# Stick-breaking sums as products of two halves: a two-layer decoder trunk on one core

## The reference

```python
z = jnp.einsum('bqhd,bkhd->bhqk', q[:, q0:kl], k[:, :kl]).astype(jnp.float32) * scale
mask = s_pos < t_pos
log_stay = jnp.where(mask, jax.nn.log_sigmoid(-z), 0.0)
between = lax.cumsum(log_stay, axis=3, reverse=True) - log_stay
a = jnp.where(mask, jnp.exp(jax.nn.log_sigmoid(z) + between), 0.0)
outs.append(jnp.einsum('bhqk,bkhd->bqhd', a.astype(v.dtype), v[:, :kl]))
...
```

## Time and profile before

| | |
|---|---|
| median of 3 runs | 1400.66 us (1398.6 to 1401.35) |
| the profiled execution | 1401.09 us, span of its instructions 1398.8 us |
| TensorE matmul busy | 1379.2 us (99%) |
| VectorE busy, ScalarE busy | 1137.6 us (81%), 933.0 us (67%) |
| TensorE's granted clock, mean | 0.995 of full |
| the two stretches with the changed steps | 64 to 112 us and 364 to 412 us |

### The profile page before, as it was taken

The page is one execution under the profiler, slowest core; times in us unless marked ns, Lnnn a source line. Parts: engine busy times, 40 slices in busy tenths (PEclk is TensorE's granted clock), DMA queues, the critical chain, the costliest instruction groups (busy, mean ns, idle before and its releaser), DMA issues.

```text
span 1398.8 us, 19126 instructions
## 1 busy us (share of the span) xinstructions
PE 1379.2 (99%) x7313; PEld 1172.1 (84%) x7313; DVE 1137.6 (81%) x872; ACT 933.0 (67%) x751; POOL 35.8 (3%) x53
## 2 busy tenths in 40 slices
PE   9999999999999999999999999999999999999986
PEld 8888999889888888888888888888888888888765
DVE  6866565556857998988888888898888888888897
ACT  5555443445645777777777777777777777777775
POOL 0010000000010020000000000000000000000200
PEclk9999999999999999999999999999999999999998
DMA  9734985546424999999999999999999999999993
GB/s 333 278 106 152 398 321 182 197 164 204 157 92 149 350 371 395 396 394 397 387 394 395 356 385 394 373 370 387 391 357 395 389 370 375 394 389 351 397 394 153
DMA packets 191039, 448.78 MB, mean 321 GB/s; under 512 B 8516, under 2 KB 11275, under 8 KB 190987
## 3 DMA queue, kind: packets, MB, share of 16 engines
q1 hardware_dynamic: 189162, 441.74, 86.1%
q0 software_dynamic: 1616, 5.77, 1.1%
q10 hardware_dynamic: 208, 0.54, 0.1%
HBM read 429.67 MB, written 18.36 MB: 320 GB/s over the span
## 4 chain that ended last, share of the span: by engine, by line
PE 88%; DVE 5%; DMA 3%; issue 1%; ACT 1%; SPq 1%; DVEq 0%; ACTq 0%
PE ps L551 81%; DVE w_lo L386 4%; DMA raw<-in_expert_w_up 2%; PE ps L1010 2%; ACT w_hi L381 1%; PE ps L682 1%; DMA raw<-in_w_in 1%; PE ps L713 0%; PE ps L969 0%; PE ps L736 0%; PE ps L640 0%; PE ps L671 0%; PE ps L556 0%; PE ps L935 0%; PE ps L980 0%
## 5 line engine op out<-in xcount | busy, mean ns | idle before, releaser
L386 DVE TENSOR_TENSOR w_lo<-raw,w_hi 128x2048 fp32r<-128x2048 f32 x401 | 914.5, 2290 | 186.7 <-ACT w_hi L381 186.0
L381 ACT ACTIVATE w_hi<-raw 128x2048 fp32r<-128x2048 f32 x400 | 766.4, 1918 | 296.5 <-PE ps L551 276.4
L551 PE MATMUL ps<-w_hi,xe_hi 128*128 128x512 f32 x896 | 244.8, 395 | 0.0
L551 PE MATMUL ps<-w_lo,xe_hi 128*128 128x512 f32 x896 | 240.1, 390 | 0.1
L551 PE MATMUL ps<-w_hi,xe_lo 128*128 128x512 f32 x896 | 240.0, 390 | 0.0
L551 PEld LDWEIGHTS ps<-w_hi,xe_lo 128*128 128x128 f32 x896 | 168.2, 188 | 35.9
L551 PEld LDWEIGHTS ps<-w_lo,xe_hi 128*128 128x128 f32 x896 | 167.9, 188 | 36.2 <-DVE w_lo L386 0.9
L551 PEld LDWEIGHTS ps<-w_hi,xe_hi 128*128 128x128 f32 x896 | 164.6, 188 | 31.7
L551 PE MATMUL ps<-w_lo,he_hi 128*128 128x512 f32 x448 | 121.4, 392 | 5.7 <-DVE w_lo L386 5.5
L551 PE MATMUL ps<-w_hi,he_hi 128*128 128x512 f32 x448 | 121.1, 391 | 0.5 <-DVE he_hi L1921 0.5
L551 PEld LDWEIGHTS ps<-w_lo,he_hi 128*128 128x128 f32 x448 | 83.4, 188 | 26.4 <-DVE w_lo L386 9.3
(11 more groups left out here) (264 smaller groups left out, 964.1 us busy)
## 6 DMA issues: line engine op xcount, KB each, us to landing
raw<-in_expert_w_gate SPq DMA_DIRECT2D x112, 1024.0 KB, 7.5
raw<-in_expert_w_up SPq DMA_DIRECT2D x112, 1024.0 KB, 7.7
raw<-in_expert_w_down SPq DMA_DIRECT2D x112, 1024.0 KB, 7.4
raw<-in_w_in SPq DMA_DIRECT2D x23, 1024.0 KB, 6.0
raw<-in_dense_w_gate SPq DMA_DIRECT2D x11, 1024.0 KB, 6.4
raw<-in_dense_w_up SPq DMA_DIRECT2D x11, 1024.0 KB, 7.2
raw<-in_dense_w_down SPq DMA_DIRECT2D x11, 1024.0 KB, 5.0
raw<-in_w_out SPq DMA_DIRECT2D x8, 1024.0 KB, 5.8
```

The costliest lines, as they stand in the source:

```text
L381: nc.scalar.activation(half_of(w_hi, n), raw[:, n % RAW, :], ACT.Copy).then_inc(hi_ready, 1)
L386: nc.vector.tensor_tensor(half_of(w_lo, n), raw[:, n % RAW, :], half_of(w_hi, n).bitcast(F32), ALU.subtract).then_inc(lo_ready, 1)
L551: return pe.matmul(o, stationary, moving, start=start, stop=stop, skip_group_check=True)
```

## The change

The constants are copied once, at the start, to fp32r (`neg_both`). A masked `spl` is split: `stay_hi(g)` on ScalarE copies it as fp32r to `spl_hi`, `stay_lo(g)` on VectorE writes `spl` minus `spl_hi` to `spl_lo`. `add_stays(g)` does eight fp32r matmuls (four of 384 and four of 128 columns, high half first) in place of four float32 ones. `spl_hi` lies in the memory of `ab`, `spl_lo` in that of `spl`. The sum of g = 0 moves behind the second half of piece 9 and `turn_weights(6, 7)`, that of g = 3 behind `values(2)`. On ScalarE `weights(1)` moves ahead of the head factors (`inverse_root`).

```diff
+                ab = sb("ab", [P, 2, 2, ZW], F32, unsplit)
+                spl = sb("spl", [P, 2, 2, ZW], F32, unsplit)
+            spl_hi = sp_("spl_hi", [P, 2, 2, ZW], F32R)
+            spl_lo = sp_("spl_lo", [P, 2, 2, ZW], F32R)
...
-                    pe.wait_ge(spm_done, PAIRS * l + g + 1)
-                    for m in range(2):
-                        bank = ps[:, (2, 4)[g % 2] + m, :]
-                        pe.matmul(bank[:, 0:ZW], neg_tri, spl[:, g % 2, m, :], start=False, stop=False, skip_group_check=True)
-                        last = pe.matmul(bank[:, P:S], neg_one, spl[:, g % 2, m, S:ZW], start=False, stop=True,
-                                         skip_group_check=True)
+                    pe.wait_ge(neg_ready, 1)
+                    for part, made in ((spl_hi, stay_hi_done), (spl_lo, stay_lo_done)):
+                        pe.wait_ge(made, PAIRS * l + g + 1)
+                        for m in range(2):
+                            pe.matmul(ps[:, (2, 4)[g % 2] + m, 0:ZW], neg_tri, part[:, g % 2, m, :], start=False, stop=False,
+                                      skip_group_check=True)
+                        for m in range(2):
+                            last = pe.matmul(ps[:, (2, 4)[g % 2] + m, P:S], neg_one, part[:, g % 2, m, S:ZW], start=False,
+                                             stop=(part is spl_lo), skip_group_check=True)
...
+                def stay_hi(g):
+
+                    act.wait_ge(spm_done, PAIRS * l + g + 1)
+                    copy(spl_hi[:, g % 2].rearrange("p h q -> p (h q)"),
+                         spl[:, g % 2].rearrange("p h q -> p (h q)")).then_inc(stay_hi_done, 1)
...
+                def stay_lo(g):
+
+                    dve.wait_ge(stay_hi_done, PAIRS * l + g + 1)
+                    V.tensor_tensor(spl_lo[:, g % 2], spl[:, g % 2], spl_hi[:, g % 2].bitcast(F32),
+                                    ALU.subtract).then_inc(stay_lo_done, 1)
...
+                    dve.wait_ge(cst_in, 16)
+                    V.tensor_copy(neg_both[:], cst[:, C_NTRI:C_NTRI + 2 * P]).then_inc(neg_ready, 1)
```

More of the change, by code:

```diff
@@ L162, in build @@
             v_df = sp_("v_df", [P, TT, HALF])
-            ab = sp_("ab", [P, 2, 2, ZW])
+            with ExitStack() as unsplit:
+                ab = sb("ab", [P, 2, 2, ZW], F32, unsplit)
+                spl = sb("spl", [P, 2, 2, ZW], F32, unsplit)
+            spl_hi = sp_("spl_hi", [P, 2, 2, ZW], F32R)
+            spl_lo = sp_("spl_lo", [P, 2, 2, ZW], F32R)
             sq_sb = ab[:].rearrange("p a h q -> p (a h q)")[:, 0:TT * HALF]
             sq_df = hn[:, :, 0:HALF]
-            spl = sp_("spl", [P, 2, 2, ZW])
             zb = hn[:].rearrange("p t (i c k) -> p (t i) c k", i=2, c=2)
@@ L189, in build @@
             att = sp_("att", [P, PAIRS, 2, ZW])
+            neg_both = sp_("neg_both", [P, 2 * P], F32R)
+            neg_tri, neg_one = neg_both[:, 0:P], neg_both[:, P:2 * P]
         with ExitStack() as phase:
@@ L256, in build @@
         ident = cst[:, C_ID:C_ID + P]
-        neg_tri = cst[:, C_NTRI:C_NTRI + P]
-        neg_one = cst[:, C_NONE:C_NONE + P]
         ones = cst[:, C_ONE:C_ONE + P]
@@ L311, in build @@
         y_got = [[sem(f"y_got{i}{t}") for t in range(TT)] for i in range(2)]
+        neg_ready, stay_hi_done, stay_lo_done = sem("neg_ready"), sem("stay_hi_done"), sem("stay_lo_done")
         out_rows, out_sent = sem("out_rows"), sem("out_sent")
@@ L794, in _ @@
                 rows_of(9, 0, tiles=(0,))
-                add_stays(0)
                 rows_of(9, 0, tiles=(1,))
@@ L798, in _ @@
                     turn_weights(j)
+                add_stays(0)
                 pe.wait_ge(mx_done, STEPS * (l + 1))
@@ L817, in _ @@
                 values(1)
+                values(2)
                 add_stays(3)
-                values(2)
                 def w_out(i, tiles=range(TT), ends=False):
@@ L1243, in _ @@
                 keep_turned(5)
+                stay_hi(0)
                 weights(0)
@@ L1249, in _ @@
                 stay_logs(2)
+                stay_hi(1)
                 split_hi(act, n0 + 13)
+                stay_hi(2)
                 act.wait_ge(pvd_done, l + 1)
                 nc.scalar.activation(sq_df, ps[:, 6:8, :], ACT.Square).then_inc(ss_done, 1)
+                weights(1)
                 act.wait_ge(head_sums, 2 * l + 1)
                 inverse_root(head_rstd[:, 0:8], head_ln[:, 0:8], head_ss[:, 0:8], 2 * HD).then_inc(head_rstd_done, 1)
-                weights(1)
                 weights(2)
@@ L1262, in _ @@
                 act.wait_ge(gC_saved, 1)
+                stay_hi(3)
                 turned(3 * l + 1, (2, 3), gC[:, 1, l:l + 1])
@@ L1629, in _ @@
                 split_lo(dve, n0 + 11)
+                stay_lo(0)
                 dve.wait_ge(piece_used, n0 + 10)
@@ L1637, in _ @@
                 softplus(2)
+                stay_lo(1)
                 split_lo(dve, n0 + 13)
+                stay_lo(2)
                 r0 = rr[:, :, :, 0]
@@ L1654, in _ @@
                 softplus(3)
+                stay_lo(3)
                 turned(3 * l + 1, (2, 3), gC[:, 1, l:l + 1])
```

## The result

The changed kernel takes 1408.8 us (median of 6 runs, 1407.3 to 1410.35), the kernel before 1400.84 (6 runs, 1398.6 to 1401.35): ratio 1.0059, 95% interval 1.0048 to 1.007. It is slower by 8 us, more than the 0.2% that this measurement can tell, and lies outside the range of the prediction. The time is that of the third rival, in which the clock falls in both layers.

A forecast was written before the change was run, and what follows sets the result against it. TensorE was taken as the bound, with almost no room on ScalarE and VectorE ahead of v_sb. Of 2.5 us a layer saved on TensorE, 0.78 arrives, 1.56 in all: 1399.1 us against the median, range 1396.8 to 1402.2.

The forecast's parts named there:

- the third rival: TensorE's clock falls at 97.2 us, behind its idle stretch: 1409 us for both layers, 1404 for one; chance 0.10.
- where TensorE stood idle for 3 us between full products it stayed at 1.00: Profile row of the kernel before, cited on whether 1.9 us of idle time ahead of values lowers the granted clock.
- 0.62 for a time without a fall: Chance given to the forecast's case, with its own range of about 1397.3 to 1401.8 us.
- the 1.9 us: New TensorE idle stretch forecast in each layer, waiting for v_sb until 97.24 us in layer 0, ahead of values(0).
- 5 us a layer, 1409 for both: Clock rival's price: values' passes 4.0 us more and the sum about 1 in each layer.
- the passes double (36 x 0.112 = 4.0 us more): Clock rival's step: three groups of values, 36 passes of 64 columns, all at the lower clock level.
- A sum costs what was put: Each split sum on TensorE was put at 1.14 us in place of 1.73, 0.59 less.
- Its two terms: Split sum's price: four fp32r matmuls of 384 columns at 0.172 us and four of 128 at 0.112.
- Two of the sum's bounds: Low ends for one fp32r matmul of the split sum: 0.160 us for 384 columns, 0.057 for 128.
- the forecast's case: Clock holds, w_out(0) begins 0.78 us earlier, 1.56 us gained in both layers: 1399.1 us against the median; chance 0.62.
- The first rival: Room on ScalarE and VectorE is larger than read, so all 5.0 us arrive: 1395.7 us; chance 0.12.
- The second, that the chain eats everything: One more 0.78 us a layer on the ScalarE and VectorE chain: 1400.7 to 1402 us; chance 0.16.

The follow-up runs named there:

- e1: Changed kernel with eight 128x128 float32 matmuls that nobody reads filling TensorE's idle stretch ahead of values(0): 1398.6 us, ratio 0.9987.
- e11: Changed kernel with four small unread products in the idle stretch ahead of values(0), leaving 1.07 us idle: 1401.4 us, ratio 1.0006.
- e3: Changed kernel with the sums of pairs 1 and 2 in float32 as before, not split: 1398.1 us, ratio 0.9984.
- e5: Changed kernel with the sum of pair 2 alone left in float32: 1397.5 us, ratio 0.999.
- e4: Changed kernel with v_sb copied ahead of stay_logs(3), and the turned rows ahead of the halves of pair 3: 1397.6 us, ratio 0.9987.
- e12: Kernel before with two small chained ScalarE copies ahead of v_sb, 1.34 us idle ahead of values(0): 1405.1 us, ratio 1.0042.
- e2: Kernel before with three small chained ScalarE copies ahead of v_sb, 2.07 us idle ahead of values(0): 1407.9 us, ratio 1.006.
- e7: Kernel before with three small chained ScalarE copies ahead of v_sb and sum 3, in float32, behind values(2): 1413.0 us, ratio 1.0097.
- e9: Changed kernel with four unread float32 products of 512 columns between the wait for v_sb and values(0): 1407.6 us, ratio 1.005.

## Why the prediction was wrong

**The step that failed** is the weighing of the third rival: "where TensorE stood idle for 3 us between full products it stayed at 1.00", and from it 0.10 for the clock, 0.62 for a time without a fall, and no term for the clock in the sum. One execution's row was read as a rule, and one that ends 0.14 us after the idle stretch, where in the changed kernel the clock came down only 1.1 to 1.5 us behind it. The runs showed in its place that the idle stretch of 1.96 us lowers the clock in both layers for 10.2 us each: 1408.8 against 1398.6 for e1. The place of that row loses its clock in 10 of 14 profiles, where a fall costs at most 1.7 us and barely shows. The Trainium skill, "TensorE: Matmul & The Clock Gate" (the part on the clock gate), says that an idle TensorE loses its clock and that the point of transition varies from run to run. The traces agree with the first by 1408.8 against 1398.6; the two heaps of e11 show more than the second, that with 1.07 us of idle time the fall itself comes in some runs only. The same page warns only of idle gaps longer than this one, so by its advice too the 1.9 us would have passed as safe; here the measurement decides. As a rival, the clock should have had the larger chance.

**The rival's price was right, in part by luck.** "5 us a layer, 1409 for both": 5.1 lost in each, 1408.8 measured. The step "the passes double (36 x 0.112 = 4.0 us more)" counted all of `values` at half clock. In fact the first dozen still ran at full clock, and for that `w_out(0)`'s first 3 us ran at half: it starts 3.55 us late (106.08 for 102.53), and the rest up to 5.1 is lost in it. The two errors cancel.

**The timeline ahead of the fall** came out as forecast. Rows of ScalarE and VectorE, for the earlier trace rows:

```profile
75.38 0.81 ACT L1214 ACTIVATE att<-ps 128x768 f32<-128x768 f32 x1 [3.26 <-PE ps L690]
...
84.44 1.90 ACT L385 ACTIVATE w_hi<-raw 128x2048 fp32r<-128x2048 f32 x1
...
96.57 1.25 ACT L1127 ACTIVATE v_sb<-ps,row_fine 128x512 f32<-128x512 f32 x2
```

```profile
86.37 2.29 DVE L390 TENSOR_TENSOR w_lo<-raw,w_hi 128x2048 fp32r<-128x2048 f32 x1 [0.71 <-ACT w_hi L385]
88.58 0.95 DVE L1555 TENSOR_TENSOR spl_lo<-spl,spl_hi 128x768 fp32r<-128x768 f32 x1
...
92.76 1.29 DVE L1679 TENSOR_TENSOR hn<-ps,scl 128x512 f32<-128x512 f32 x2
93.97 0.95 DVE L1542 TENSOR_SCALAR ab<-ps 128x768 int32<-128x768 int32 x1
```

- `weights(0)` at 75.38 (forecast 75.44), the split of piece 13 at 84.44 (84.56), its low half at 86.37 (86.50).
- `stay_lo(2)` pushes the scaled rows to 92.76 (92.67); `minus_abs(3)` has no idle time ahead of it and starts at 93.97 (93.88), `v_sb` at 96.57 (96.50) without a wait for TensorE, `values(0)` at 97.29 (97.24) behind 1.96 us of idle time (1.9).
- A sum costs what was put: with a piece behind it 1.18 us from its first matmul to that of the piece, 85.41 to 86.59 (forecast 1.14). Its two terms were each off and cancel: by the distances between starts, two products of 384 columns take 0.43 and 0.41, two of 128 take 0.17, so about 0.21 and 0.085 for one, where 0.172 and 0.112 had been put. Whether the weight loads hold the short ones isn't shown by this.

```profile
85.41 0.59 PE L687 MATMUL ps<-spl_hi,neg_both 128*128 128x384 f32 x2
85.84 0.33 PE L690 MATMUL ps<-spl_hi,neg_both 128*128 128x128 f32 x2
86.01 0.57 PE L687 MATMUL ps<-spl_lo,neg_both 128*128 128x384 f32 x2
86.42 0.33 PE L690 MATMUL ps<-spl_lo,neg_both 128*128 128x128 f32 x2
86.59 1.14 PE L555 MATMUL ps<-w_hi,aT_hi 128*128 128x512 f32 x4
```

- Two of the sum's bounds don't follow from their working: by the slope of 0.118 and 0.227 against zero 384 columns take 0.164 and not 0.160, and half of 0.118 is 0.059 and not 0.057. Neither moves the forecast.
- With the clock held, e1, the gain of the forecast's case is there: 1398.6 for 1399.1. The first rival, the full gain of 5 us, is out, since TensorE does wait 1.96 us for `v_sb`; the versions without that wait, or with 0.46 us of it, gain 2.3 to 2.9 (in e3 and e5 fewer sums are split, in e4 another wait of 0.61 us stands at sum 3). The second, that the chain eats everything, is out as well by e1.

**Open.** What decides, at 1 to 2 us of idle time, whether a given execution loses its clock; why the stretches at the lower level last 3.4, 6.8 or 10.2 us behind the same code (layer 0 of e12, e2 and the changed kernel all go on to `values`); and the 5.1 us between e2 and e7. More profiles of one and the same kernel would help, and weren't taken. Part of the spread of all kernels, the kernel before too (1398.3 to 1402.4), may come from such falls at the place of the earlier trace rows and in the stage around 431 to 440 us; that is argued and not shown.

## What to carry to other kernels

A change that shortens TensorE's work in a stretch where the others have no room turns the saving into idle time, and on TensorE that isn't free: 1.96 us of it cost 5 us a layer here with passes of 64 columns behind it, and 1.7 with wide products (e9). So price a new idle stretch with the work behind it, and treat a single row in which the clock held as one draw; look at the same place in several traces first. If the stretch can't be closed by reordering what is waited for (e4) or by taking work off the chain (e3, e5), filling it with products that nobody reads won the 10 us of the two falls back (e1).

## What the runs showed of the hardware

- In the changed kernel and e9, work behind the stretch made the difference in how long the clock stays low: 10.2 us with `values` behind it, 3.4 with 3.5 us (at full clock) of 512-column products, for the same 1.96 us of idle time.
- GpSimd was slowed beside the new `stay_lo`. Two of its mask steps (two instructions each), 0.77 us in the kernel before, took 1.42 and 1.31 us where they met VectorE's instructions with two inputs in SBUF (`stay_lo(1)` runs from 84.71 to 85.66, `stay_lo(2)` from 88.58 to 89.53); rows of GpSimd in the changed kernel:

```profile
84.86 1.42 POOL L500 TENSOR_SCALAR_AFFINE_SELECT spl<-spl 128x256 f32<-128x256 f32 x2 [2.84 <-DVE spl L1549]
88.85 1.31 POOL L500 TENSOR_SCALAR_AFFINE_SELECT att<-att 128x256 f32<-128x256 f32 x2 [2.56 <-ACT att L1214]
```

This agrees with the Trainium skill, "SBUF — State Buffer", by which GpSimd and VectorE hold one pair of ports in turns. VectorE's small instruction at 89.45 paid for it as well, 0.37 us for 0.16. Nothing waited for the masks, but those 0.2 us of VectorE lie in the chain that ends in `v_sb`, and so in the 1.96 us of idle time.
